# Latent attention with the softmax exponentials issued one head earlier on ScalarE, the query scaling and the spreading of the sums moved there from GpSimd, and finer waits ahead of the scores

## The chip, the cores and the metric

The program runs on one core of one Trainium2 chip. The metric is the device time in microseconds of that core for one execution of the whole program. A core has five engines that each work through a queue of their own in program order: TensorE (PE in the profile, with its weight loads as PEld), VectorE (DVE), ScalarE (ACT), GpSimd (POOL) and SyncE (SP, which issues DMAs). They wait for each other by semaphores.

## The reference, cut to what matters

Two transformer blocks follow each other on a sequence of 1024 tokens of width 1024, all in float32. The change lies in one stage of the second block, the attention over the latent tokens and 256 context tokens:

```
h  = modulate(rmsnorm(x), shift, scale)               # 1024 tokens; hc the same for 256 context tokens
q  = rope(rmsnorm(h @ Wq) * g_q)                      # 8 heads of 128
k, v = those of hc and h, one after the other         # 1280 keys, 2 key heads of 128
for each block of 128 queries and each head:
    s = (q @ k.T) / sqrt(128)                         # 128 x 1280
    y = softmax(s) @ v
```

The projections ahead of this stage and behind it, the two mixers of the first block, the pooling mixer and the feed-forward parts are not touched.

## The kernel before

Products on TensorE are taken in three parts: each float32 operand is split into a high part, which TensorE reads as it is, and a low part, what is left; high x high, high x low and low x high are added up in PSUM. So whatever is transposed on TensorE is read twice from PSUM: by ScalarE, which writes the high part (a copy that rounds), and then by VectorE, which subtracts it and so gives the low part.

The function `latent_attention` (L1298) walks over 8 tiles of 128 queries (`walk`, L1351: the first and the last tile written out, the six between as a hardware loop) and in each over 8 heads. The heads have a running number n from 0 to 63. Two halves of PSUM, three banks each, serve even and odd heads in turn: a half holds first the 1280 scores of its head, and then, in the same banks, the ten transposed 128x128 blocks of its probabilities, in three groups of 4, 4 and 2 blocks. What each engine does for head n, in its order:

- TensorE: transposes the probabilities of head n (L1409), for even heads also the spread reciprocals of the sums (L1402); then one half of the product with the values for the pair of heads before (L1427 to L1429, 15 matmuls); then the scores of head n+2 (`scores`, L1384; its matmuls are L1393 to L1395) in three parts of 512, 512 and 256 keys, which overwrite the banks of the transposed probabilities of head n. For that it waits on the semaphore `probs_t_dve`: before the first part until VectorE has written low groups 0 and 1 of head n, before the third until it has written group 2.
- ScalarE: writes the high parts of the three groups of head n (L1555), for even heads with the copy of the turned factors (L1542) between groups 1 and 2; then the exponentials of head n+1 (`exps`, L1527, its instruction L1531), whose maximum has been there for most of a head.
- VectorE: for odd n the reciprocal of the sums (L1615); the low parts of the three groups (L1629); now and then a piece of the next tile's queries; for odd n the product with the factors (L1620); then the largest score of head n+2 and its negative (L1609, L1611).
- GpSimd: for odd n, the reciprocals spread over 128 columns (`spread_sums`, L1494, its instruction L1498).

The queries of the next tile are made ready on the side, piece by piece: squares on ScalarE in head 0 (L1537), sums on VectorE in head 1 (L1581), the reciprocal root (L1466, L1469) and the scaling of the rows by it (`query_scale`, L1471, L1477) on GpSimd in head 2, the gain on VectorE in head 3 (L1592), the rotation on VectorE and GpSimd in heads 4 and 5 (L1597, L1598, L1604; L1483, L1484, L1492). In head 6 TensorE transposes them in two lots of four heads (`turn_queries`, L1372, its instruction L1381), through one bank: the second lot waits until ScalarE (L1525) and VectorE (L1576) have taken the first, and the scores of the next tile's first head wait for both.

Of the kernel before, what the change touches and what calls it, by code (L numbers as in the profile page):

```python
# [15 lines left out]
ALU = mybir.AluOpType  # L16
ACT = mybir.ActivationFunctionType
# [5 lines left out]
TILES = 8  # L23
# [10 lines left out]
HD2 = 128  # L34
QH2, KV2 = 8, 2
# [172 lines left out]
def bcast(ap, n):  # L208

    return ap.unsqueeze(2).broadcast_to([ap.shape[0], ap.shape[1], n])  # L210
# [1087 lines left out]
def latent_attention(core, q, columns, gain, gain_dram, rotary, kT_hi, kT_lo, v, v_low, ahead):  # L1298
# [15 lines left out]
    with ExitStack() as st:  # L1314
# [18 lines left out]
        with nc.Block() as block:  # L1333
# [28 lines left out]
            def pair_of(t, h):  # L1362
                return t * (QH2 // 2) + h // 2 - 1
# [7 lines left out]
            def _(pe):  # L1371
# [12 lines left out]
                def scores(pe, n, t, h, first=False):  # L1384
                    if h % 4 == 0:
                        pe.wait_ge(core.kq_out_dve.sem, core.kq_out_dve.at(2 * t + 1 + h // 4))
                    g = h // rep
                    for part, (a, b) in enumerate(PARTS):
                        if not first and part != 1:

                            pe.wait_ge(core.probs_t_dve.sem, core.probs_t_dve.at(3 * (n - 2) + (2 if part == 0 else 3)))
                        out = s_bank(h % 2)[:, a:b]
                        nc.tensor.matmul(out, qT_hi[:, h], kT_hi[:, g, a:b], start=True, stop=False)  # L1393
                        nc.tensor.matmul(out, qT_hi[:, h], kT_lo[:, g, a:b], start=False, stop=False)
                        last = nc.tensor.matmul(out, qT_lo[:, h], kT_hi[:, g, a:b], start=False, stop=True)  # L1395
                    last.then_inc(core.scores.sem, 1)
# [63 lines left out]

            @block.gpsimd
            def _(pool):
                def query_rstd(t):
                    pool.wait_ge(core.sums.sem, core.sums.at(t + 1))
                    pool.nop(nofuse=True)
                    pool.tensor_scalar(qrs[:], qsum[:], 1.0 / HD2, EPS, ALU.mult, ALU.add).then_inc(core.links_pool.sem, 1)  # L1466
                    pool.wait_ge(core.links_pool.sem, core.links_pool.at(t + 1))
                    pool.nop(nofuse=True)
                    pool.tensor_tensor(qrs[:], qrs[:], core.minus_half[:, 0:QH2], ALU.pow).then_inc(core.rstd.sem, 1)  # L1469

                def query_scale(t):  # L1471
                    row3, scaled3 = (x.rearrange("p (h d) -> p h d", d=HD2) for x in (q(t), scaled[:]))
                    pool.wait_ge(core.rstd.sem, core.rstd.at(t + 1))
                    pool.nop(nofuse=True)
                    pool.wait_ge(core.rot_dve.sem, core.rot_dve.at(3 * t))
                    pool.nop(nofuse=True)
                    pool.tensor_tensor(scaled3, row3, bcast(qrs[:], HD2), ALU.mult).then_inc(core.hidden.sem, 1)  # L1477

                def query_turn(t):
                    cos, sin = turn_tables(rotary, t, QH2)  # L1480
                    pool.wait_ge(core.staged.sem, core.staged.at(t + 1))
                    pool.nop(nofuse=True)
                    pool.tensor_tensor(product[2][:], b_in, cos, ALU.mult).then_inc(core.rot_pool.sem, 1)  # L1483
                    pool.tensor_tensor(product[3][:], a_in, sin, ALU.mult).then_inc(core.rot_pool.sem, 1)  # L1484

                def query_turned(t):
                    pool.wait_ge(core.rot_pool.sem, core.rot_pool.at(2 * t + 2))
                    pool.nop(nofuse=True)
                    if not isinstance(t, int) or t > 0:
                        pool.wait_ge(core.kq_turned.sem, core.kq_turned.at(2 * t))  # L1490
                        pool.nop(nofuse=True)
                    pool.tensor_tensor(b_out, product[2][:], product[3][:], ALU.add).then_inc(core.kq_rows.sem, 1)  # L1492

                def spread_sums(p, s):  # L1494
                    pool.wait_ge(core.links_dve.sem, core.links_dve.at(p + 1))
                    pool.nop(nofuse=True)
                    for x in range(2):
                        last = pool.tensor_scalar(spread[:, x], core.ones[:], rtotal[:, 2 * s + x:2 * s + x + 1], None, ALU.mult)  # L1498
                    last.then_inc(core.one_over.sem, 1)

                def tile(pool, t, first, more):
                    for h in range(QH2):
                        if more and h == 2:
                            query_rstd(t + 1)
                            query_scale(t + 1)
                        if more and h == 4:
                            query_turn(t + 1)
                        if more and h == 5:
                            query_turned(t + 1)
                        if h % 2:  # L1510
                            spread_sums(pair_of(t, h) + 1, (h // 2) % 2)
                query_rstd(0)
                query_turn(0)
                query_turned(0)
                pool.wait_ge(core.values_high.sem, core.values_high.at(1))
                pool.nop(nofuse=True)
                pool.tensor_tensor(v_low[:], v, v_hi[:].bitcast(F32), ALU.subtract).then_inc(core.values_low.sem, 1)
                walk(pool, tile)
                ahead.first_splits(pool)

            @block.scalar
            def _(act):
                def q_high(act, t, c):
                    act.wait_ge(core.kq_turned.sem, core.kq_turned.at(2 * t + c + 1))
                    act.activation(qT_hi[:, 4 * c:4 * c + 4], q_bank, ACT.Copy).then_inc(core.kq_hi.sem, 1)  # L1525

                def exps(act, n, h):  # L1527

                    act.wait_ge(core.mins.sem, core.mins.at(n + 1))
                    b, q4 = h % 2, h % 4  # L1530
                    act.activation(pr[:, b], s_bank(b)[:, 0:KEYS], ACT.Exp, bias=nb[:, b:b + 1], scale=SCALE,  # L1531
                                   accum_out=total[:, q4:q4 + 1]).then_inc(core.probs.sem, 1)

                def query_squares(t):
                    if not isinstance(t, int) or t > 0:
                        act.wait_ge(core.sums.sem, core.sums.at(t))
                    act.activation(squares[:], q(t), ACT.Square).then_inc(core.sq.sem, 1)  # L1537

                def take_factors(p):
                    if not isinstance(p, int) or p > 0:  # L1540
                        act.wait_ge(core.heads_out.sem, core.heads_out.at(p))
                    act.activation(factors[:], factor_bank, ACT.Copy).then_inc(core.parts_act.sem, 1)  # L1542

                def tile(act, t, first, more):
                    for h in range(QH2):
                        n = t * QH2 + h
                        some = not (first and h < 2)
                        for g in range(3):
                            act.wait_ge(core.probs_t.sem, core.probs_t.at(3 * n + g + 1))
                            if g == 0 and not (first and h < 4):  # L1550

                                act.wait_ge(core.pv.sem, core.pv.at(pair_of(t, h)))
                            if g == 2 and some and h % 2 == 0:
                                take_factors(pair_of(t, h))
                            act.activation(pt(pT_hi, h, g), by_tiles(pt_bank(h % 2, g)), ACT.Copy).then_inc(core.probs_t_act.sem, 1)  # L1555
                        if more or h + 1 < QH2:
                            exps(act, n + 1, (h + 1) % QH2)
                        if more and h == QH2 - 2:
                            q_high(act, t + 1, 0)
                            q_high(act, t + 1, 1)  # L1560
                        if more and h == 0:
                            query_squares(t + 1)
                query_squares(0)
                act.activation(v_hi[:], v, ACT.Copy).then_inc(core.values_high.sem, 1)
                q_high(act, 0, 0)
                q_high(act, 0, 1)
                exps(act, 0, 0)
                walk(act, tile)
                act.wait_ge(core.probs_t.sem, core.probs_t.at(3 * heads + 1))
                take_factors(heads // 2 - 1)  # L1570
# [81 lines left out]
    n = heads  # L1652
# [1973 lines left out]
```

## Time and profile before

| | us |
|---|---|
| device time, median of 3 runs | 3812.06 |
| lowest and highest of the 3 | 3809.18, 3813.14 |
| the profiled execution's own time | 3812.06 |
| its span, first to last instruction | 3810.3 |

Busy over the whole span: TensorE 91%, its weight loads 80%, VectorE 58%, ScalarE 46%, GpSimd 37%. These are means over many stages with different limits; the stage of the change lies between about 1737 and 2104 us of the span. "Idle before" in a row is the time in which the engine did nothing ahead of that row, and the name behind the arrow is what ended it.

### The profile page before, as it was taken

How to read it: one execution, taken by the hardware profiler on the slowest of the kernel's cores; microseconds unless marked ns; L12 is line 12 of the kernel's file. 1: busy time of each engine (PE TensorE's matmuls, PEld its weight loads, DVE VectorE, ACT ScalarE, POOL GpSimd, SP SyncE). 2: the span in 40 equal slices, each digit the busy share in tenths (PEclk: the TensorE clock that was granted, in tenths of full speed). 3: DMA queues.
4: the chain of work that ended last, by engine and by line, in shares of the span. 5: the costliest groups of instructions: out<-in, count | busy, mean ns of one | idle time of the engine just before them, and what ended most of it. 6: DMA issues, size and time to landing. Idle time of an engine off the chain costs nothing. (4 is left out here: it accounts for less than half of the span.)

```text
span 3810.3 us, 59174 instructions
## 1 busy us (share of the span) xinstructions
PE 3464.8 (91%) x18690; PEld 3042.7 (80%) x18690; DVE 2214.7 (58%) x4502; ACT 1740.2 (46%) x4132; POOL 1401.2 (37%) x1828
## 2 busy tenths in 40 slices
PE   5999988899999999797999929999999949999998
PEld 4899877899999987586888727888787748888786
DVE  5466767355677775435777175666435566666334
ACT  1277511667777771324555153333334463333333
POOL 2365323455566763313331334444001224444000
PEclk8999989899999998898999959999999769999999
DMA  3311255211122214300000022222354012222354
GB/s 145 127 40 39 101 221 220 87 42 42 59 62 64 63 61 160 129 1 28 1 0 0 22 107 76 83 83 83 127 197 150 29 49 83 83 83 83 127 198 143
DMA packets 97166, 332.99 MB, mean 87 GB/s; under 512 B 10673, under 2 KB 37601, under 8 KB 85090
## 3 DMA queue, kind: packets, MB, share of 16 engines
q1 hardware_dynamic: 96994, 330.90, 24.5%
q8 instruction: 83, 1.36, 0.2%
q14 instruction: 89, 0.73, 0.1%
HBM read 269.76 MB, written 61.10 MB: 87 GB/s over the span
## 5 line engine op out<-in xcount | busy, mean ns | idle before, releaser
L2062 PE MATMUL ps<-down_high,hidden_high 128*128 128x512 f32 x704 | 277.3, 394 | 13.5 <-DVE hidden_low L1963 13.2
L2045 PE MATMUL ps<-columns_combined,up_high_even 128*128 128x512 f32 x616 | 243.7, 396 | 46.4 <-POOL up_low_even L1830 32.7
L2063 PE MATMUL ps<-down_low,hidden_high 128*128 128x512 f32 x704 | 275.8, 392 | 0.0
L2064 PE MATMUL ps<-down_high,hidden_low 128*128 128x512 f32 x704 | 275.5, 391 | 0.0
L374 PE MATMUL ps<-w_hi,hT_hi 128*128 128x512 f32 x640 | 254.2, 397 | 22.5 <-DVE hT_lo L398 11.9
L1961 DVE TENSOR_TENSOR down_low<-down_raw,down_high 128x1024 fp32r<-128x1024 f32 x88 | 107.8, 1225 | 273.4 <-ACT down_high L1878 273.4
L375 PE MATMUL ps<-w_lo,hT_hi 128*128 128x512 f32 x640 | 252.8, 395 | 0.0
L376 PE MATMUL ps<-w_hi,hT_lo 128*128 128x512 f32 x640 | 252.1, 394 | 0.0
L2046 PE MATMUL ps<-columns_combined,up_high_even 128*128 128x512 f32 x616 | 242.9, 394 | 0.0
L2047 PE MATMUL ps<-columns_combined,up_low_even 128*128 128x512 f32 x616 | 242.5, 394 | 0.0
L2046 PE MATMUL ps<-columns_combined,up_high_odd 128*128 128x512 f32 x616 | 239.7, 389 | 0.0
L2047 PE MATMUL ps<-columns_combined,up_low_odd 128*128 128x512 f32 x616 | 239.7, 389 | 0.0
L2045 PE MATMUL ps<-columns_combined,up_high_odd 128*128 128x512 f32 x616 | 239.7, 389 | 0.0
L1089 ACT ACTIVATE masked_then_probs<-masked_then_probs,unit_rows 128x256 f32<-128x256 f32 (+1 forms) x512 | 229.1, 451 | 3.2 <-DVE sink_term L1176 1.8
L1878 ACT ACTIVATE down_high<-down_raw 128x1024 fp32r<-128x1024 f32 x88 | 93.1, 1058 | 269.6 <-PE ps L2064 257.2
L1026 PEld LDWEIGHTS ps<-v_tiles,probsT 128*128 128x128 f32 x1600 | 203.4, 198 | 1.3 <-issue 1.3
L971 PE MATMUL ps<-w_units,hT_hi 128*128 128x384 f32 (+1 forms) x512 | 184.7, 361 | 18.3 <-DVE w_units L1135 12.5
L1026 PE MATMUL ps<-v_tiles,probsT 128*128 128x64 f32 x1600 | 199.9, 277 | 0.6 <-DVE unit_rows L1249 0.6
L973 PE MATMUL ps<-w_units,hT_lo 128*128 128x384 f32 (+1 forms) x576 | 199.4, 346 | 0.0
L1167 DVE CUSTOM_DVE_ANT_0 masked_then_probs<-ps,mask 128x256 f32<-128x256 f32 (+1 forms) x512 | 156.2, 359 | 60.5 <-PE ps L988 60.1
L2460 DVE SCALAR_TENSOR_TENSOR mod_sums<-mod_weights,silu_c,mod_sums 128x512 f32 x196 | 184.7, 954 | 6.0
L971 PE MATMUL ps<-w_units,hT_hi_by_fours 128*128 128x384 f32 (+1 forms) x512 | 183.6, 359 | 0.2 <-ACT z L1116 0.2
(365 smaller groups left out, 9999.4 us busy)
## 6 DMA issues: line engine op xcount, KB each, us to landing
mod_weights<-in_w_mod SPq DMA_DIRECT2D x24, 2048.0 KB, 8.5
up_raw<-in_w_up SPq DMA_DIRECT2D x44, 1024.0 KB, 4.8
down_raw<-in_w_down SPq DMA_DIRECT2D x88, 512.0 KB, 3.6
hidden_columns<-hidden SPq DMA_DIRECT2D x44, 512.0 KB, 2.6
hidden_columns<-hidden_columns SPq DMA_DIRECT2D x88, 256.0 KB, 3.9
w_raw<-in_w_in_b SPq DMA_DIRECT2D x24, 768.0 KB, 4.5
group_rows<-unit_rows SPq DMA_DIRECT2D x64, 132.0 KB, 1.8
unit_rows<-group_rows SPq DMA_DIRECT2D x64, 132.0 KB, 2.1
```

The lines of the kernel that those rows point to most:

```text
L374: nc.tensor.matmul(out, a, w_hi[:, s], start=(k == 0), stop=False)
L375: nc.tensor.matmul(out, a, w_lo[:, s], start=False, stop=False)
L376: last = nc.tensor.matmul(out, b, w_hi[:, s], start=False, stop=(k == KT - 1))
L971: nc.tensor.matmul(zbank, hi, weights(w_hi, a.unit, k), start=(k == 0), stop=False)
L1026: last = nc.tensor.matmul(o_bank[:, h * HD:(h + 1) * HD], pT[:, a.par, h, c], vs[:, tile], start=(c == a.slots[0]), stop=(c == a.slots[-1]))
L1089: act.activation(x, x, ACT.Exp, bias=own, scale=-1.0, accum_out=total).then_inc(core.probs.sem, 1)
L2045: nc.tensor.matmul(out, a_hi, combined.moving(0, z, k), start=(start and k == 0), stop=False, **again)
L2046: nc.tensor.matmul(out, a_hi, combined.moving(1, z, k), start=False, stop=False, **again)
L2047: last = nc.tensor.matmul(out, a_lo, combined.moving(0, z, k), start=False, stop=(k == 3), **again)
L2062: nc.tensor.matmul(out, h_hi[:, s, t], down_hi[:, s, cols], start=begin, stop=False)
L2063: nc.tensor.matmul(out, h_hi[:, s, t], down_lo[:, s, cols], start=False, stop=False)
L2064: last = nc.tensor.matmul(out, h_lo[:, s, t], down_hi[:, s, cols], start=False, stop=end)
```

## The change

Four things are changed, all in `latent_attention`.

1. `exps` is issued one head earlier. ScalarE starts with the exponentials of heads 0 and 1, and in head n, behind the high parts of head n, it issues those of head n+2 in place of those of head n+1. In head 6 the high parts of the turned queries now stand ahead of the exponentials.
2. The scaling of the queries moves from GpSimd (one instruction, 128x1024) to ScalarE (eight instructions of 128x128, each with its head's scale), into head 2 behind the exponentials.
3. The spreading of the reciprocals moves from GpSimd to ScalarE, into odd heads between the high parts and the exponentials. GpSimd is left with the reciprocal root and its part of the rotation, without the walk over heads; it also comes earlier to the first splits of the next projection's weights.
4. The scores wait for `probs_t_dve` before each of the three parts: for low group 0, 1 and 2 in turn.

```diff
@@ scores, TensorE
                     for part, (a, b) in enumerate(PARTS):
-                        if not first and part != 1:
-
-                            pe.wait_ge(core.probs_t_dve.sem, core.probs_t_dve.at(3 * (n - 2) + (2 if part == 0 else 3)))
+                        if not first:
+
+                            pe.wait_ge(core.probs_t_dve.sem, core.probs_t_dve.at(3 * (n - 2) + part + 1))
@@ GpSimd
-                def query_scale(t):
...
-                    pool.tensor_tensor(scaled3, row3, bcast(qrs[:], HD2), ALU.mult).then_inc(core.hidden.sem, 1)
...
-                def spread_sums(p, s):
...
-                walk(pool, tile)
+                with pool.Fori(1, TILES) as t:
+                    queries(t)
                 ahead.first_splits(pool)
@@ ScalarE
+                def query_scale(t):
+                    act.wait_ge(core.rstd.sem, core.rstd.at(t + 1))
+                    act.wait_ge(core.rot_pool.sem, core.rot_pool.at(2 * t))
+                    act.wait_ge(core.rot_dve.sem, core.rot_dve.at(3 * t))
+                    act.nop(nofuse=True)
+                    for h in range(QH2):
+                        last = act.activation(scaled[:, h * HD2:(h + 1) * HD2], q(t)[:, h * HD2:(h + 1) * HD2], ACT.Copy, scale=qrs[:, h:h + 1])
+                    last.then_inc(core.hidden.sem, 1)
+
+                def spread_sums(p, s):
+                    act.wait_ge(core.links_dve.sem, core.links_dve.at(p + 1))
+                    for x in range(2):
+                        last = act.activation(spread[:, x], core.ones[:], ACT.Copy, scale=rtotal[:, 2 * s + x:2 * s + x + 1])
+                    last.then_inc(core.one_over.sem, 1)
@@ ScalarE, tile, at the end of head h
-                        if more or h + 1 < QH2:
-                            exps(act, n + 1, (h + 1) % QH2)
+                        if h % 2:
+                            spread_sums(pair_of(t, h) + 1, (h // 2) % 2)
                         if more and h == QH2 - 2:
                             q_high(act, t + 1, 0)
                             q_high(act, t + 1, 1)
+                        if more or h + 2 < QH2:
+                            exps(act, n + 2, (h + 2) % QH2)
                         if more and h == 0:
                             query_squares(t + 1)
+                        if more and h == 2:
+                            query_scale(t + 1)
@@ ScalarE, ahead of the walk
                 exps(act, 0, 0)
+                exps(act, 1, 1)
```

ScalarE's queue in heads 1 to 3 of the first tile, before: `probsT_high` are the high parts, `probs,sums` the exponentials. The two rows of `probs,sums` are the exponentials of heads 2 and 3.

```order
L1555 ACTIVATE probsT_high<-ps 128x4x128 [waits probs_t] x2
L1555 ACTIVATE probsT_high<-ps 128x2x128 [waits probs_t]
L1531 ACTIVATE probs,sums<-ps,minus_largest 128x1280 [waits mins]
L1555 ACTIVATE probsT_high<-ps 128x4x128 [waits probs_t] x2
L1542 ACTIVATE factors_by_query<-ps 128x256 [waits probs_t]
L1555 ACTIVATE probsT_high<-ps 128x2x128
L1531 ACTIVATE probs,sums<-ps,minus_largest 128x1280 [waits mins]
L1555 ACTIVATE probsT_high<-ps 128x4x128 [waits probs_t] x2
```

The same place in the changed kernel, where line numbers differ; the rows of `probs,sums` are now the exponentials of heads 3 and 4.

```order
L1540 ACTIVATE probsT_high<-ps 128x2x128 [waits probs_t]
L1521 ACTIVATE one_over_sums_spread<-ones,one_over_sums 128x128 [waits links_dve]
L1521 ACTIVATE one_over_sums_spread<-ones,one_over_sums 128x128
L1501 ACTIVATE probs,sums<-ps,minus_largest 128x1280 [waits mins]
L1540 ACTIVATE probsT_high<-ps 128x4x128 [waits probs_t] x2
L1527 ACTIVATE factors_by_query<-ps 128x256 [waits probs_t]
L1540 ACTIVATE probsT_high<-ps 128x2x128
L1501 ACTIVATE probs,sums<-ps,minus_largest 128x1280 [waits mins]
L1515 ACTIVATE scaled_queries<-x,query_rstd 128x128 [waits rot_dve,rstd,rot_pool]
L1515 ACTIVATE scaled_queries<-x,query_rstd 128x128 x7
L1540 ACTIVATE probsT_high<-ps 128x4x128 [waits probs_t] x2
```

The order of high parts and exponentials is the same in shape, but each exponential belongs to one head later, and spreading and scaling now stand in the same queue.

TensorE's scores of one head in the changed kernel, first tile. Before, the second row of 128x512 with L1393 had no wait, and the rest reads the same.

```order
L1393 MATMUL ps<-kT_hi,qT_hi 128x512 [waits probs_t_dve]
L1394 MATMUL ps<-kT_lo,qT_hi 128x512
L1395 MATMUL ps<-kT_hi,qT_lo 128x512
L1393 MATMUL ps<-kT_hi,qT_hi 128x512 [waits probs_t_dve]
L1394 MATMUL ps<-kT_lo,qT_hi 128x512
L1395 MATMUL ps<-kT_hi,qT_lo 128x512
L1393 MATMUL ps<-kT_hi,qT_hi 128x256 [waits probs_t_dve]
```

There is one wait more in a head's scores, and the first asks for one low group where it asked for two.

## Rows read from the trace of the kernel before

**Rows 1.** Stretch view: one tile; busy time of each engine, then PEclk.
```profile
core 0: us, PE busy (x) PEld busy (x) DVE busy (x) ACT busy (x) POOL busy (x), PEclk, DMA share, GB/s
...
1932.02:1975.42 43.40, 40.63 (x290) 36.94 (x289) 33.58 (x56) 24.58 (x47) 12.34 (x14) 1.00 0.00 0
```

**Rows 2.** View of waits, 1760 to 2100 us: who waited for whom, in total.
```profile
ACT probsT_high L1555 <- PE ps L1409: 134.7, 64, 2.6
...
PEld ps L1393 <- DVE probsT_low L1629: 22.2, 45, 2.2
...
PEld ps L1381 <- DVE qT_lo L1576: 10.0, 7, 1.4
```

**Rows 3.** Timeline of the first heads: start, duration, engine, line, operation, count, idle before.
```profile
1756.90 1.49 DVE L1609 TENSOR_REDUCE largest<-ps 128x1 f32<-128x1280 f32 x1 [1.88 <-PE ps L1395]
...
1758.43 0.15 DVE L1611 TENSOR_SCALAR minus_largest<-largest 128x1 f32<-128x1 f32 x1
1758.62 1.33 ACT L1531 ACTIVATE probs<-ps,minus_largest 128x1280 f32<-128x1280 f32 x1 [4.32 <-DVE minus_largest L1611]
...
1760.21 0.15 DVE L1611 TENSOR_SCALAR minus_largest<-largest 128x1 f32<-128x1 f32 x1
1760.79 1.36 ACT L1555 ACTIVATE probsT_high<-ps 128x512 fp32r<-128x512 f32 x3 [0.75 <-PE ps L1409]
1761.41 1.62 DVE L1629 TENSOR_TENSOR probsT_low<-ps,probsT_high 128x512 fp32r<-128x512 f32 x3 [1.05 <-ACT probsT_high L1555]
...
1762.76 0.50 PE L1393 MATMUL ps<-kT_hi,qT_hi 128*128 128x512 f32 x1 [1.35 <-DVE probsT_low L1629]
...
1764.81 1.49 DVE L1609 TENSOR_REDUCE largest<-ps 128x1 f32<-128x1280 f32 x1 [1.78 <-PE ps L1395]
```

**Rows 4.** Timeline, head 6 of a tile, ScalarE's own.
```profile
1920.19 1.09 ACT L1555 ACTIVATE probsT_high<-ps 128x512 fp32r<-128x512 f32 x2 [2.56 <-PE ps L1409]
...
1921.68 1.36 ACT L1531 ACTIVATE probs<-ps,minus_largest 128x1280 f32<-128x1280 f32 x1
...
1922.99 0.63 ACT L1525 ACTIVATE qT_hi<-ps 128x512 fp32r<-128x512 f32 x1
```

**Rows 5.** Timeline, heads 0 and 1: squares on ScalarE, VectorE's odd head.
```profile
1891.93 1.09 ACT L1537 ACTIVATE query_squares<-x 128x1024 f32 x1
...
1895.85 1.62 DVE L1629 TENSOR_TENSOR probsT_low<-ps,probsT_high 128x512 fp32r<-128x512 f32 x3
...
1898.51 0.41 DVE L1620 TENSOR_TENSOR x<-ps,factors_by_query 128x256 f32 x1
```

**Rows 6.** Timeline of ScalarE in other stages: small scaled activations.
```profile
905.78 1.29 ACT L1069 ACTIVATE scaled<-z,head_rstd 128x64 f32<-128x64 f32 x5
906.97 0.46 ACT L1077 ACTIVATE squares<-z 128x320 f32<-128x320 f32 x1
...
3080.00 2.88 ACT L3074 ACTIVATE pool_columns<-ps,modulation,pre_gain_ffn 128x128 f32<-128x128 f32 x8
```

**Rows 7.** Timeline, head 6: the turned queries' low part and TensorE.
```profile
1923.64 0.69 DVE L1576 TENSOR_TENSOR qT_lo<-ps,qT_hi 128x512 fp32r<-128x512 f32 x1 [0.70 <-ACT qT_hi L1525]
...
1924.39 0.66 PE L1381 MATMUL ps<-identity,q_rows 128*128 128x128 f32 x4 [1.24 <-DVE qT_lo L1576]
1924.80 0.48 PE L1393 MATMUL ps<-kT_hi,qT_hi 128*128 128x512 f32 x1
```

**Rows 8.** Timeline: the last two heads' high parts.
```profile
2092.94 1.09 ACT L1555 ACTIVATE probsT_high<-ps 128x512 fp32r<-128x512 f32 x2 [2.35 <-PE ps L1409]
...
2096.62 1.36 ACT L1555 ACTIVATE probsT_high<-ps 128x512 fp32r<-128x512 f32 x3 [0.74 <-PE ps L1409]
```

**Rows 9.** Stretches of 4 us, columns as in rows 1.
```profile
1764.00:1768.00 4.00, 2.06 (x16) 1.75 (x15) 3.15 (x7) 3.09 (x6) 1.20 (x2) 1.00 0.00 0
...
2924.00:2928.00 4.00, 4.00 (x12) 3.15 (x11) 3.97 (x4) 0.00 (x0) 0.00 (x0) 0.57 0.88 267
```

**Rows 10.** Timeline of TensorE: after an idle time, and the very first scores.
```profile
2923.38 0.50 PE L2062 MATMUL ps<-down_high,hidden_high 128*128 128x512 f32 x1 [2.91 <-DVE hidden_low L1963]
...
1753.32 0.78 PE L1393 MATMUL ps<-kT_hi,qT_hi 128*128 128x512 f32 x1
```

More of the change, by code:

```diff
@@ L1462, in _, with queries @@
             def _(pool):
-                def query_rstd(t):
+                def queries(t, first=False):
+                    cos, sin = turn_tables(rotary, t, QH2)
                     pool.wait_ge(core.sums.sem, core.sums.at(t + 1))
@@ L1469, in query_rstd @@
                     pool.tensor_tensor(qrs[:], qrs[:], core.minus_half[:, 0:QH2], ALU.pow).then_inc(core.rstd.sem, 1)
-                def query_scale(t):
[L1472 to L1476, printed above, removed]
-                    pool.tensor_tensor(scaled3, row3, bcast(qrs[:], HD2), ALU.mult).then_inc(core.hidden.sem, 1)
-                def query_turn(t):
-                    cos, sin = turn_tables(rotary, t, QH2)
                     pool.wait_ge(core.staged.sem, core.staged.at(t + 1))
@@ L1484, in query_turn @@
                     pool.tensor_tensor(product[3][:], a_in, sin, ALU.mult).then_inc(core.rot_pool.sem, 1)
-                def query_turned(t):
                     pool.wait_ge(core.rot_pool.sem, core.rot_pool.at(2 * t + 2))
                     pool.nop(nofuse=True)
-                    if not isinstance(t, int) or t > 0:
+                    if not first:
                         pool.wait_ge(core.kq_turned.sem, core.kq_turned.at(2 * t))
@@ L1492, in query_turned @@
                     pool.tensor_tensor(b_out, product[2][:], product[3][:], ALU.add).then_inc(core.kq_rows.sem, 1)
-                def spread_sums(p, s):
[L1495 to L1514, printed above, removed]
+                queries(0, first=True)
                 pool.wait_ge(core.values_high.sem, core.values_high.at(1))
```

## The prediction

> **What bounds the kernel now.** I read the stage by stretches first. One whole tile of eight heads takes 43.40 us, 5.43 us a head; TensorE is busy for 40.63 us of it, 5.08 us a head, at full clock (1.00), and ScalarE for 24.58 only [rows 1]. So TensorE is nearly the bound, and ScalarE has room as a sum. The view of waits says what TensorE's idle time is: in some 340 us its weight loads wait 22.2 us for the low parts ahead of the scores, and 10.0 us at the turned queries [rows 2]. Some 32 us in the whole stage are all that better waits could give. ScalarE's largest wait is 134.7 us, for the transposed probabilities: today it stands ready when TensorE delivers. The reader is to ask of the change whether it still will.
>
> For that the first heads are of use, since nothing covers their steps there, and the chain can be read step by step [rows 3]: largest at 1756.90, its negative at 1758.43, exponentials at 1758.62; high parts at 1760.79, low parts at 1761.41, scores at 1762.76, next largest at 1764.81.
>
> **The change, part by part.**
>
> *The exponentials one head earlier.* In the changed queue the exponentials of head n+2 stand ahead of the high parts of head n+1. They need the largest score of head n+2, and this needs its scores, which TensorE writes just ahead of transposing head n+1. Before, the exponentials at this place had their maximum long since. Now ScalarE waits there with the high parts of head n+1 behind it; VectorE's low parts wait for those, and the scores of head n+3 for the low parts, which closes a loop with one turn a head. What stands in each queue behind the wait is thus the next link of the same loop, and no other work can come forward.
>
> The rule that decides is in the Trainium skill, "TensorE: Matmul & The Clock Gate", section on architectural detail: the queues of ScalarE and VectorE are strictly first in, first out. Were it not so, the high parts could pass the waiting exponentials and the loop would not close; that is the third rival below. The rows show the order kept and no case that would have tempted it.
>
> One turn of the loop, from start to start:
> - scores to largest: 1762.76 to 1764.81, 2.05 [rows 3]
> - largest to its negative: 1756.90 to 1758.43, 1.53 [rows 3]
> - negative to exponentials: 1758.43 to 1758.62, 0.19 [rows 3]
> - exponentials with the reading of their sum, to the next work in the queue: 1921.68 to 1922.99, 1.31 [rows 4]
> - first high part to first low part: 1760.79 to 1761.41, 0.62 [rows 3]
> - first low part to the scores: before, two low groups took 1761.41 to 1762.76, 1.35 [rows 3]; with the finer wait one is enough, 0.69 long by rows 7's instruction of the same shape plus 0.06 to reach TensorE (1923.64 + 0.69 to 1924.39), 0.75 [rows 7]. The later groups follow at the pace of the score parts and cost nothing.
>
> The sum is 6.45 us a head, against 5.08 of work on TensorE, which is left with 1.37 idle. So the finer waits save 0.60 a turn, but inside a loop that is 1.4 longer per head than TensorE's work.
>
> The high parts of head 0 come after both first exponentials: the second can start at 1760.21 + 0.19 = 1760.40 and ends its turn 1.31 later at 1761.71, against 1760.79 before [rows 3]: +0.92. From there to the high parts of head 62 are 62 turns: 62 x 6.45 = 399.9.
>
> *Side work that now stands in the loop*, once for each of the seven next tiles:
> - the squares in head 0 come between exponentials and high parts: 1.09 long, less the overlap of about 0.1 that neighbours in the queue have, 1.0 [rows 5].
> - the scaling, eight activations with a scale by pointer, stands at the same place in head 2. The row of 128x64 gives 5 in 1.19, 0.238 each (905.78 to 906.97) [rows 6], a lower end of 1.90; 128x128 from PSUM with two pointers gives 2.88/8 = 0.36, an upper end of 2.88 [rows 6]. Each column more costs (1.36 - 0.63) / 768 = 0.95 ns, by the exponentials of 1280 and the copy of 512 columns [rows 4]; I take the lower end plus 64 such columns: 0.30 each, 2.39. GpSimd's root and its wait are over by then.
> - the turning of queries in head 6: counted from the first high part of head 6, ScalarE comes to the queries after 1.49 (1920.19 to 1921.68), the first lot takes 0.63 [rows 4], VectorE 0.75 to TensorE and the second lot 0.41 (1924.39 to 1924.80) [rows 7]; with 0.05 for a handover, the scores of the next tile start at 3.33 instead of 0.62 + 0.75 = 1.37: +1.96. The exchange that puts the high parts of the queries ahead of the exponentials is needed for this, and otherwise hidden.
> - VectorE in heads 1, 3 and 4: low parts, a query piece and the product take 1895.85 to 1898.51 and 0.41 more [rows 5], so the largest can start 0.62 + 2.66 + 0.41 = 3.69 after the first high part, where the loop wants it at 0.62 + 0.75 + 2.05 = 3.42: +0.27, three times 0.81.
>
> Together 6.16, times seven 43.1. Spreading the sums (two activations, under 0.4 each by the same rows) costs nothing: it falls into ScalarE's wait for the largest. If the loop were not there it would cost 0.6 in odd heads on an engine that is half idle. GpSimd's relief saves nothing that TensorE waits for, and its splits for the next projection come earlier without being wanted.
>
> *The end.* Head 63 has no exponentials between it and head 62, so its high parts follow after 1.49 [rows 4] where 2092.94 to 2096.62 is 3.68 now [rows 8]: -2.19.
>
> Heads 0 to 62 took 1760.79 to 2092.94, 332.15 [rows 3, 8]. The sum is 0.92 + 399.9 + 43.1 - 332.15 - 2.19 = +109.6.
>
> *TensorE's clock.* After an idle time of 2.91 TensorE started at 2923.38 [rows 10], and the next 4 us show a granted clock of 0.57 although it was busy throughout: mostly the lower level, 1.2 GHz [rows 9]. In the stretch 1764 to 1768 it idled 1.94 of 4 us and kept 1.00, 2.4 GHz [rows 9]. The changed loop idles 1.37 in a plain head, 2.4 at the squares, 3.8 at the scaling and up to 3.3 at the queries, so falls are likely at two places a tile. Cold scores take 1753.32 to 1756.90, 3.58 [rows 3, 10], 1.53 more than 2.05; since the fall in rows 9 comes a good half microsecond after the restart, I take 0.95 a fall: 7 x 2 x 0.95 = 13.3. Bounds: 0, and three whole ones a tile, 32.
>
> All this is against the profiled execution: its own time, 3812.06, has 1.76 outside the span and is also the median of the runs shown. 3812.1 + 109.6 + 13.3 = 3935.0, the forecast. Its own range is 3905 (scaling at 1.90, VectorE never late, no fall of the clock: 3812.1 + 109.6 - 3.4 - 5.7 = 3912.6, and 0.1 less a head for handovers that overlap) to 3965 (32 for the clock, 3.4 for the scaling at 0.36, 0.1 more a head for the loop's register instructions).
>
> **Rivals.**
>
> *The clock falls in every head.* For it: 2.91 of idle sufficed, and no row shows a steady 1.37 in 6.45. Against it: 1.94 idle within 4 us did no harm. Price: 1.53 in each of 62 turns in place of 13.3: 3921.7 + 95 = 4017; if it goes to and fro, half of it, 3969. The Trainium skill, same page, section on the clock gate, has only two levels, and a clock that activity releases. By that rule the price would be all or nothing at each restart; the granted 0.57 and 1.00 of rows 9 agree with two levels.
>
> *Only the loop costs, the side work hides.* If squares, scaling and queries fell into waits: 3812.1 + 0.92 + 399.9 - 332.15 - 2.19 = 3878.6. Against it: they stand between the exponentials and the high parts, where ScalarE is the link of the loop.
>
> *The exponentials don't hold the high parts back.* Then TensorE stays the bound and the finer waits give what they can: 22.2 less ahead of the scores [rows 2], 3790, faster. The place is ScalarE's queue between two heads, and the point that decides is whether 3.03 us (1.53 + 0.19 + 1.31) from the largest to the end of the exponentials fit before the first transposed block is there. TensorE transposes at once behind the scores, and the largest waits for the same scores, so the first transposed block is there while VectorE still looks for the largest; they don't fit. Only if the scores came a head ahead would this hold, and their banks don't allow that.
>
> **How the numbers follow.** The forecast 0.72; the clock in every head or most 0.16; hidden side work 0.06; the faster rival 0.05; anything else 0.01. The predicted time is that of the first. The range reaches down to 3895, for a loop that is shorter than its steps, and up to 3990, past the half of the clock rival, and leaves out less than 2 in 10. About 0.2% is what a measurement of this kernel can tell from no change, 7.6 us; only the third rival lies on the other side: faster 0.05, same 0.01, slower 0.94.
>
> **What would show it.** The first high part of one head to that of the next should be 6.4 to 6.5 us in plain heads (5 and 7), over 7 behind squares and over 8.5 behind the scaling; a tile about 57.8 us (8 x 6.45 + 6.16) plus what the clock takes. ScalarE's largest wait should be for the negative of the largest, where it was for the transposed probabilities, each about 3 to 3.7 us (6.45 less 1.49 for the high parts, 1.31 for the exponentials and up to 0.6 for spreading); the wait of the scores for the low parts should grow from 22.2 to over 80 us, with TensorE's busy time in the stage hardly changed. Granted clock under 1.00 should show behind the scaling. I am wrong if the high parts start while exponentials are outstanding, if plain heads take 5.1 to 5.4 us, or if TensorE idles elsewhere than ahead of the scores.

## The result, and the profile after

| | before | changed |
|---|---|---|
| device time, median of 4 runs | 3810.62 us | 3929.35 us |
| lowest to highest | 3808.26 to 3813.14 | 3924.3 to 3935.17 |
| ratio, with its 95% interval | | 1.0312 (1.0294 to 1.033) |
| span of the profiled execution | 3810.3 us | 3935.0 us |
| the profiled execution's own time | 3812.06 us | 3936.82 us |

The changed kernel is 3.1% slower. The forecast was 3935 with a range of 3895 to 3990. The profiled execution of the changed kernel took 7.5 us more than the median of its other four; the traces below are of that one.

The stretch view of the changed kernel shows one tile, from the first high part of head 7 to that of the next head 7, and single heads of it; columns as in rows 1.

```profile
1935.94:1942.38 6.44, 5.07 (x36) 4.62 (x36) 3.60 (x6) 3.25 (x9) 0.00 (x0) 1.00 0.00 0
...
1965.19:1972.94 7.75, 6.39 (x36) 5.88 (x36) 4.73 (x7) 3.23 (x9) 3.82 (x3) 0.78 0.00 0
...
1935.94:1994.23 58.29, 42.25 (x288) 38.24 (x288) 33.20 (x55) 29.11 (x66) 5.66 (x5) 0.97 0.00 0
```

A tile takes 58.29 us where it took 43.40 [rows 1]. TensorE is busy 42.25 us of it, hardly more than the 40.63 before; most of the 1.6 more is the head at a granted clock of 0.78, busy for 6.39 where the plain head shows 5.07. ScalarE's 29.11 against 24.58 is the work moved to it. Neither engine is full; what grew is waiting. A plain head (first row) lasts 6.44 us.

The view of waits of the changed kernel, 1760 to 2215 us, in the form of rows 2:

```profile
ACT probs L1501 <- DVE minus_largest L1601: 223.7, 62, 5.0
DVE probsT_low L1619 <- ACT probsT_high L1540: 141.6, 62, 4.2
...
PEld ps L1393 <- DVE probsT_low L1619: 107.7, 53, 4.1
...
PEld ps L1381 <- DVE qT_lo L1566: 18.6, 7, 2.7
```

Read downwards this is the loop: the exponentials wait for the largest (62 times, 3.6 us each), the low parts for the high parts behind them, the scores for the low parts, 107.7 us where it was 22.2 [rows 2]. ScalarE's wait for the transposed probabilities, 134.7 us before, is gone from the list: now TensorE has delivered long since, and the high parts lie in the queue.

ScalarE's timeline of the changed kernel through most of that tile (heads 7, 0, 1, 2, 3), columns as in rows 3:

```profile
1935.94 1.35 ACT L1540 ACTIVATE probsT_high<-ps 128x512 fp32r<-128x512 f32 x3
1937.16 0.71 ACT L1521 ACTIVATE one_over_sums_spread<-ones,one_over_sums 128x128 f32<-128x128 f32 x2
1941.06 1.33 ACT L1501 ACTIVATE probs<-ps,minus_largest 128x1280 f32<-128x1280 f32 x1 [3.19 <-DVE minus_largest L1601]
...
1942.38 1.07 ACT L1540 ACTIVATE probsT_high<-ps 128x512 fp32r<-128x512 f32 x2
...
1948.82 1.04 ACT L1507 ACTIVATE query_squares<-x 128x1024 f32 x1
1949.76 1.35 ACT L1540 ACTIVATE probsT_high<-ps 128x512 fp32r<-128x512 f32 x3
...
1956.40 1.07 ACT L1540 ACTIVATE probsT_high<-ps 128x512 fp32r<-128x512 f32 x2
...
1962.86 2.43 ACT L1515 ACTIVATE scaled_queries<-x,query_rstd 128x128 f32 x8
1965.19 1.33 ACT L1540 ACTIVATE probsT_high<-ps 128x512 fp32r<-128x512 f32 x3
...
1972.94 1.08 ACT L1540 ACTIVATE probsT_high<-ps 128x512 fp32r<-128x512 f32 x2
```

From one first high part to the next: 6.44 (plain), 7.38 (squares between), 6.64, 8.79 (scaling between), 7.75 (no work between, but granted clock 0.78). High parts never start while an exponential is outstanding ahead of them. The spreading sits in front of ScalarE's 3.19 us wait and costs nothing.

TensorE's timeline in the changed kernel, the starts of scores that had to wait:

```profile
1943.75 0.50 PE L1393 MATMUL ps<-kT_hi,qT_hi 128*128 128x512 f32 x1 [1.36 <-DVE probsT_low L1619]
1951.13 0.50 PE L1393 MATMUL ps<-kT_hi,qT_hi 128*128 128x512 f32 x1 [2.52 <-DVE probsT_low L1619]
...
1966.55 0.55 PE L1393 MATMUL ps<-kT_hi,qT_hi 128*128 128x512 f32 x1 [3.90 <-DVE probsT_low L1619]
```

1.36 idle in a plain head, 2.52 behind the squares, 3.90 behind the scaling.

### The profile page after: what moved, and what is told of

The parts are those of the page before. It is cut to its first block and busy times, and to the rows that moved or that the text cites. A ratio compares the mean times of both kernels' runs of the same rounds, so it can differ in the third digit from the quotient of the medians.

```text
span 3935.0 us, 59284 instructions
## 1 busy us (share of the span) xinstructions
PE 3494.9 (89%) x18690; PEld 3066.0 (78%) x18690; DVE 2218.2 (56%) x4502; ACT 1774.3 (45%) x4252; POOL 1347.6 (34%) x1757
## 3 DMA queue, kind: packets, MB, share of 16 engines
q8 instruction: 83, 1.36, 0.1%
## 5 line engine op out<-in xcount | busy, mean ns | idle before, releaser
L1501 ACT ACTIVATE probs<-ps,minus_largest 128x1280 f32<-128x1280 f32 x64 | 85.2, 1330 | 231.3 <-DVE minus_largest L1601 231.3
```

## The experiments

Eight kernels took the change apart or shifted one part of it; two more look for a better order. They ran in three groups, each with runs of the kernel before beside it, whose medians were 3813.0, 3808.5 and 3812.7 us; a ratio is always to the kernel before of the same group.

**The exponentials alone.** The kernel before with this edit (and the exponentials of head 1 ahead of the walk):

```diff
-                        if more or h + 1 < QH2:
-                            exps(act, n + 1, (h + 1) % QH2)
                         if more and h == QH2 - 2:
                             q_high(act, t + 1, 0)
                             q_high(act, t + 1, 1)
+                        if more or h + 2 < QH2:
+                            exps(act, n + 2, (h + 2) % QH2)
```

> The kernel before with one part of the change alone: the exponentials one head earlier (heads 0 and 1 ahead of the walk, the turned queries' high parts ahead of the exponentials in head 6). Scaling, spreading and the coarse waits stay as before. Theory of the loop: a plain head lasts 6.44 as in the changed kernel plus 0.60 for the coarser wait, 7.04; squares add 1.0 and the queries 1.36 per tile; 62 x 7.04 + 7 x 2.36 against 332.15 before gives +120, with about 13 for the clock 3943 us, between 3930 and 3975. Rival, the loss comes from the scaling and spreading put on ScalarE: close to before, 3800 to 3820.

Measured: 3953.39 us, ratio 1.0373 (1.0358 to 1.0388). A plain head, in ScalarE's timeline of this kernel:

```profile
1909.51 1.35 ACT L1555 ACTIVATE probsT_high<-ps 128x512 fp32r<-128x512 f32 x3
...
1916.57 1.07 ACT L1555 ACTIVATE probsT_high<-ps 128x512 fp32r<-128x512 f32 x2
```

1909.51 to 1916.57 is 7.06 us, as the loop wants it. This one part makes a loss larger than the whole change's. The 10 us above the expected 3943 are largely the clock's: in this trace 23 heads show a granted clock below 1.00 and are 25 us longer in all than heads of their kind at 1.00, where 13 had been taken.

**The finer waits alone.** The kernel before with the first hunk of the change.

> The kernel before with the three finer waits ahead of the scores alone. Theory of the loop: waits for low parts are only 22.2 us before, and the first score part may start one low group, 0.60, earlier; so 10 to 22 us faster, 3789 to 3800. Rival, the added wait costs something or another engine is late at once: 3805 to 3815.

Measured: 3789.67 us, ratio 0.9945 (0.9933 to 0.9957). The loads' wait for low parts fell from 22.2 to 4.9 us; the 10.0 us at the turned queries stayed. A tile takes 40.6 us (1922.62 to 1963.21) where it took 43.40. The rival falls.

**All but the exponentials.** The changed kernel, with the exponentials back:

```diff
-                        if more or h + 2 < QH2:
-                            exps(act, n + 2, (h + 2) % QH2)
+                        if more or h + 1 < QH2:
+                            exps(act, n + 1, (h + 1) % QH2)
```

> The changed kernel with the exponentials back at their old place (those of head n+1 behind the high parts of head n), while scaling and spreading stay on ScalarE and the waits stay fine. Theory of the loop: plain heads fall to TensorE's 5.0 to 5.2 us, the whole to 3790 to 3812. Rival, ScalarE's added work makes the loss: it stays above 3870.

Measured: 3786.67 us, ratio 0.9933 (0.9921 to 0.9945). A tile of this kernel:

```profile
1932.45:1972.68 40.23, 39.36 (x289) 36.59 (x288) 33.68 (x56) 29.24 (x65) 5.69 (x5) 1.00 0.00 0
```

ScalarE's busy time is that of the changed kernel (29.24 and 29.11), yet the tile takes 40.23 us instead of 58.29, and TensorE is busy 98% of it. So it is not the amount of work on ScalarE, but the place of the exponentials, that makes the loss. With the finer waits this kernel is even faster than the one before. Its interval overlaps with that of the finer waits alone (0.9933 to 0.9957), so with the exponentials at their old place the scaling and the spreading on ScalarE cost nothing that can be told.

**The exponentials between the groups.** The changed kernel with the exponentials of head n+1 behind group 0, and then behind group 1, of the high parts of head n:

```diff
                             act.activation(pt(pT_hi, h, g), by_tiles(pt_bank(h % 2, g)), ACT.Copy).then_inc(core.probs_t_act.sem, 1)
+                            if g == 0 and (more or h + 1 < QH2):      # second kernel: g == 1
+                                exps(act, n + 1, (h + 1) % QH2)
```

> The changed kernel with the exponentials of head n+1 between the first and second group of the high parts of head n, so one group of high parts later than in the changed kernel. Theory of the loop: only score parts 2 and 3 hang on the exponentials now, the first part of 0.70 us leaves the loop: plain heads of 6.44 - 0.70 = 5.74 us, squares and scaling hidden, the whole 3840 to 3860. Rival, ScalarE is late as a whole by what was added to its queue: no change against the changed kernel, 3925 to 3935.

> The changed kernel with the exponentials of head n+1 between the second and third group of the high parts of head n. Theory of the loop: only the last score part (0.35 us) hangs on them, a turn of 4.6 to 4.8 us is shorter than TensorE's work of 5.08, so TensorE is the bound again: 3785 to 3805. Rival, any wait of ScalarE for a fresh maximum ahead of high parts holds TensorE back: over 3820.

Measured: 3857.05 us, ratio 1.0114 (1.0098 to 1.0129), behind group 0; 3801.9 us, ratio 0.9985 (0.9976 to 0.9994), behind group 1. ScalarE's timeline, behind group 0:

```profile
1939.32 0.60 ACT L1540 ACTIVATE probsT_high<-ps 128x512 fp32r<-128x512 f32 x1 [2.02 <-PE ps L1409]
1940.64 1.33 ACT L1501 ACTIVATE probs<-ps,minus_largest 128x1280 f32<-128x1280 f32 x1 [0.71 <-DVE minus_largest L1600]
...
1945.19 0.60 ACT L1540 ACTIVATE probsT_high<-ps 128x512 fp32r<-128x512 f32 x1 [1.80 <-PE ps L1409]
1946.39 1.33 ACT L1501 ACTIVATE probs<-ps,minus_largest 128x1280 f32<-128x1280 f32 x1 [0.60 <-DVE minus_largest L1600]
```

The first group's high part now stands ahead of the exponentials and is no link of the loop, so the turn is read from one exponential to the next: 1940.64 to 1946.39, 5.75 us, where 5.74 was expected. In the last tile, which prepares no queries, the seven turns are 5.74 to 5.76 us.

Behind group 1, two heads of the last tile in the stretch view, and VectorE in a head with a piece of the next queries (the rotation):

```profile
2066.87:2076.33 9.46, 9.46 (x73) 8.77 (x72) 6.93 (x13) 6.42 (x14) 0.00 (x0) 1.00 0.00 0
```

```profile
1909.71 0.42 DVE L1618 TENSOR_TENSOR probsT_low<-ps,probsT_high 128x256 fp32r<-128x256 f32 x1 [0.78 <-ACT probsT_high L1540]
1910.05 0.68 DVE L1586 TENSOR_TENSOR rotation<-scaled_queries,axial 128x512 f32<-128x512 f32 x1
1910.65 0.69 DVE L1587 TENSOR_TENSOR rotation<-scaled_queries,axial 128x512 f32<-128x512 f32 x1
1911.25 1.48 DVE L1598 TENSOR_REDUCE largest<-ps 128x1 f32<-128x1280 f32 x1
```

Plain heads take 6.44 us with the exponentials ahead of all groups, 5.75 behind the first, and 4.73 behind the second (9.46 for two), where TensorE is busy throughout (less than the 5.08 us a head that the prediction read from a whole tile); with the exponentials at their old place a pair of plain heads takes 9.45 us in the last tile. So the loop shrinks by what no longer hangs on it, until TensorE's own work is longer.

Still this order stays 15 to 20 us (by medians and by ratios) behind the old place with the same waits. The loss lies in the seven tiles that prepare queries: one takes 42.44 us (1882.62 to 1925.06) against 40.23, and seven times 2.2 is 15.5. From head 1 to head 5 of that tile the exponentials follow each other at 5.15 to 5.25 us. In one of these four turns ScalarE is busy throughout, with the scaling. In the others VectorE has a query piece; in the rows above it waits 0.78 us for the high part behind the exponentials, and then goes through the low part, the piece and the next largest without a pause. So a smaller loop between ScalarE and VectorE is left, and the expected rival holds in part.

**The coarse waits back.** The changed kernel without its first hunk.

> The changed kernel with the old coarse waits ahead of the scores. Theory of the loop: each turn is longer by a low group of 0.60: 7.04 in plain heads, 62 x 0.60 = 37 less what it saves where VectorE or the queries are late (about 4 a stage each): 3955 to 3975. Rival, the waits don't matter since ScalarE sets the pace: no change, 3929.

Measured: 3970.78 us, ratio 1.0421 (1.0405 to 1.0437), by the medians 41 us over the changed kernel. Plain heads take 7.05 us (1926.79 to 1933.84 on ScalarE), 0.61 more. Not every turn pays that: the head of the turned queries keeps its 8.38 us, and behind squares and scaling 7.05 stands against 6.64. That makes some 31 us in 62 heads; the clock takes most of the rest, as 25 heads below 1.00 lose 27 us in this trace against 18 heads and 18 us in that of the changed kernel. In the kernel before the same edit was worth 23 us against its group's median, since there it removed only waits.

**The scaling back on GpSimd.** The changed kernel with the one instruction of 128x1024 behind the root on GpSimd, in place of the eight on ScalarE.

> The changed kernel with the scaling of the queries alone back on GpSimd as one instruction of 128x1024. Theory of the loop: 2.35 less per tile and, with that idle time gone, no fall of the clock behind it (1.0 per tile): 7 x 3.35 = 23 us faster than the changed kernel, 3906; the head behind head 2 lasts 6.44 to 6.7. Rival, the scaling hides in ScalarE's wait for the largest: no change, 3929.

Measured: 3905.25 us, ratio 1.0253 (1.0238 to 1.0269), 24 us less than the changed kernel. The head that held the scaling takes 6.45 us (1941.07 to 1947.52 on ScalarE), the one behind it 6.65. The rival falls: work between exponentials and high parts is paid in full. The clock still falls behind the squares in four of the seven tiles, as it does in the changed kernel; one tile that shows it:

```profile
1933.12:1941.07 7.95, 6.59 (x36) 5.87 (x36) 4.72 (x7) 3.24 (x9) 3.74 (x3) 0.79 0.00 0
1947.52:1954.17 6.65, 5.10 (x36) 4.62 (x36) 4.64 (x7) 3.25 (x10) 2.77 (x3) 1.00 0.00 0
```

In the two traces the stage differs by 30.0 us (461.98 against 491.94): seven times 2.34 for the scaling, and 13.5 because the clock fell in 6 heads where it fell in 18. The medians lie only 24 us apart, and the profiled execution of the changed kernel was a long one; so how often the clock falls seems to differ between executions of one kernel, which no further trace here shows.

**TensorE kept busy behind the scaling.** The changed kernel with this:

```diff
+                        if more and h == 3:
+                            for n_ in range(28):
+                                nc.tensor.transpose(q_bank[:, n_ % 4], core.ident[:], core.ident[:])
                         if more or h + 2 < QH2:
                             scores(pe, n + 2, t + (h + 2) // QH2, (h + 2) % QH2)
```

> The changed kernel with 28 extra transposes of the identity on TensorE (about 3 us) into the unused query bank, ahead of the scores of head 3, where TensorE idles 3.8 us behind the scaling. Their results are not used. If the clock makes the head behind the scaling 7.75 us long instead of 6.44 + 0.27: it falls to about 6.7, some 1 us a tile or 7 us in all, 3922, with a granted clock of 1.00 there. If it is VectorE or the rows' own noise: no change in that head.

Measured: 3921.51 us, ratio 1.0294 (1.0278 to 1.0309). The median is 7.8 us under that of the changed kernel, but the two intervals overlap, so what is shown is shown by the trace. TensorE's transposes and its next scores, ScalarE's timeline around the scaling, and the stretch of the head behind it:

```profile
1960.43 3.22 PE L1447 MATMUL ps<-identity 128*128 128x128 f32 x28
1964.49 0.50 PE L1393 MATMUL ps<-kT_hi,qT_hi 128*128 128x512 f32 x1 [0.84 <-DVE probsT_low L1622]
```

```profile
1960.80 2.43 ACT L1518 ACTIVATE scaled_queries<-x,query_rstd 128x128 f32 x8
1963.14 1.32 ACT L1543 ACTIVATE probsT_high<-ps 128x512 fp32r<-128x512 f32 x3
...
1969.77 1.07 ACT L1543 ACTIVATE probsT_high<-ps 128x512 fp32r<-128x512 f32 x2
```

```profile
1963.14:1969.77 6.63, 5.58 (x41) 4.88 (x39) 4.64 (x7) 3.23 (x8) 2.77 (x3) 1.00 0.00 0
```

The same head takes 6.63 instead of 7.75 us and the granted clock is 1.00 instead of 0.78. So 1.12 us of that head were the clock's, and 0.19 VectorE's. It is so in every tile: all seven heads behind the scaling take 6.63 or 6.64 us at 1.00, where in the changed kernel all seven are below 1.00 and take 6.86 to 8.00.

**Better orders.** Two kernels keep the old place of the exponentials and the finer waits, and put the high part of the first lot of queries ahead of the exponentials in head 6, that of the second lot behind them; the first leaves scaling and spreading on GpSimd, the second has them on ScalarE.

```diff
                         if more and h == QH2 - 2:
                             q_high(act, t + 1, 0)
                         if more or h + 1 < QH2:
                             exps(act, n + 1, (h + 1) % QH2)
+                        if more and h == QH2 - 2:
                             q_high(act, t + 1, 1)
```

> The kernel before with the three finer waits, and in head 6 the high part of the first lot of turned queries ahead of the exponentials (of the old place), that of the second lot behind them. With the finer waits alone TensorE still waits 10.0 us for the turned queries in seven tiles; the exponentials, 1.31, leave that wait. Expected 7 x 1.3 = 9 us less than the finer waits alone, 3781, between 3776 and 3786. Rival, TensorE then waits for the exponentials of head 7 at once: no gain, 3790.

> The changed kernel with the exponentials at their old place and, in head 6, between the two lots of the turned queries' high parts instead of behind both. With both lots ahead, TensorE waits 5.2 us in all for exponentials and 4.5 us for the queries; the former should go. Expected 3 to 6 us less than with both lots ahead (3786.7), 3780 to 3784. Rival, the second lot is late in its turn and TensorE waits there as long: no gain.

Measured: 3785.47 us, ratio 0.9933 (0.9919 to 0.9947), and 3779.31 us, ratio 0.9923 (0.9909 to 0.9936). In the second the loads' wait for exponentials fell from 5.2 to 2.3 us. It is the fastest kernel run here, 33 us under its group's median of the kernel before; its interval overlaps with the one of all but the exponentials, so by the medians the split of the two lots alone is not shown to gain. The first gained 4 us where 9 were expected, and its interval overlaps with that of the finer waits alone as well. The traces are clearer: from the exponentials of one head to those of the same head in the next tile are 39.8 us in both kernels, with the finer waits alone 40.6 and in all but the exponentials 40.2, in each of the tiles between the first and the last. In the first kernel the loads' wait at the turned queries fell only from 10.0 to 4.5 us, not to nothing as the expected 9 us would need.

## Why the prediction was right

The mechanism was the one forecast, and its steps can be set beside the trace of the changed kernel.

- *The loop's turn*: forecast 6.45, measured 6.44. The rows of the first heads gave every link, since they had run there without cover. With the coarse wait, 0.60 more by the forecast, a plain head took 7.05 and 7.06.
- *Squares, scaling, queries*: forecast 1.0, 2.39 and 1.96; measured 0.94 (7.38 - 6.44), 2.33 (1962.86 to 1965.19) and 1.95 (the last head of the tile, 1985.84 to 1994.23, less 6.44). The lengthening of the small activations from a narrower row was sound.
- *VectorE late in heads 1, 3 and 4*: forecast 0.27 each; measured 0.20 and 0.19 in heads 1 and 3, nothing in head 4 of that tile, though the prediction had counted its two products like the others without a row for them. Together 3 us too much in the stage. One head 4 was late all the same, where GpSimd, freed by the change, already splits the next projection's weights; the prediction had put that at nothing. VectorE's two products (before the dots in the usual tile, behind them in this one, with one of GpSimd's splits) took 1.12 and 1.76 us instead of 0.68 and 0.69, and the head 7.90 us (2149.95 to 2157.85) at a granted clock of 1.00, 1.45 more; with GpSimd's work left as it was (the exponentials alone) the same head took 7.05 like its plain ones. The rows show this; what slowed the two instructions was not tested.

```profile
1975.10 0.68 DVE L1587 TENSOR_TENSOR rotation<-scaled_queries,axial 128x512 f32<-128x512 f32 x1
1975.69 0.69 DVE L1588 TENSOR_TENSOR rotation<-scaled_queries,axial 128x512 f32<-128x512 f32 x1
...
2152.11 1.12 DVE L1587 TENSOR_TENSOR rotation<-scaled_queries,axial 128x512 f32<-128x512 f32 x1
2152.82 1.53 POOL L249 TENSOR_TENSOR w_lo<-w_raw,w_hi 128x512 fp32r<-128x512 f32 x1
2153.15 1.76 DVE L1588 TENSOR_TENSOR rotation<-scaled_queries,axial 128x512 f32<-128x512 f32 x1
```

- *The clock*: forecast 14 falls at 0.95, 13.3 us. The trace shows a granted clock below 1.00 in 18 of 62 heads: seven of seven behind the scaling, six of seven at the turned queries, four of seven behind the squares, and the first head. Set against heads of their kind at 1.00 they are 18.3 us longer in all, 1.02 each. At the two places that the prediction named, scaling and queries, 13 falls cost 13.1 us, as forecast. What it left out are the falls behind the squares (4.3 us) and in the first head (1.0), so the term is 5 us too small.
- *The sum*: from the first high part (1759.99) to that of head 62 (2218.89) are 458.9 us, against 456.3 forecast (443.0 without the clock). The clock is 5.0 more and the GpSimd head 1.45; VectorE's lateness is 3.0 less, squares, scaling and queries together 0.8 less. That the total fits to 3 us is thus partly luck, since misses of both signs met. In the two profiled executions the stage, from ScalarE's first squares to its first copy of the next stage, lasts 491.94 (1735.87 to 2227.81) and 368.03 us (1737.74 to 2105.77); the difference is 123.9, where 122.9 was forecast. The median of the runs lies 5.7 under the forecast. Four executions of the changed kernel differ by 11 us, but so do those of the kernel before, by 13 us in eleven, so nothing can be read from that.
- *The rivals*: the clock didn't fall in every head; all plain heads show 1.00. Nor did a restart cost all or nothing, as the prediction had drawn from the two levels: the seven heads behind the scaling lost from 0.2 to 1.4 us, each running in part at either level (granted clock 0.57 to 0.79 over the head). The side work did not hide, as the scaling on GpSimd shows. ScalarE's strict queue, which the Trainium skill gives under "TensorE: Matmul & The Clock Gate", section on architectural detail, held in every row: three places of the exponentials in the queue gave three lengths of a head.
- *The finer waits*: taken as worth up to 22 us if TensorE stayed the bound; alone they gave 23 against their group's median (21 by the ratio 0.9945).

## What to carry to other kernels

In a queue that is strictly in order, issuing an instruction earlier makes everything behind it wait for that instruction's operands: before moving one ahead, ask what it will wait for there, and whether what stands behind it feeds, through other engines, the next turn of the same wait. If so, add up the loop from rows where its links ran uncovered, and compare it with the busiest engine's work per turn; work put between two links is then paid in full, however idle its engine is. The finer waits paid in either kernel here, 23 us where TensorE was the bound and 41 in the loop.

## What the runs showed that was not expected

Extra work made a head shorter: some 3 us of transposes without a use took 1.12 us off the head that followed, because TensorE then met the scores at the full clock. Over the seven tiles that is 6.6 us, as the seven heads had lost from 0.2 to 1.4 us each; the medians differ by 7.8, though the intervals don't separate the two kernels.

The same idle time does not always end the same way. In the changed kernel TensorE is idle 2.52 us ahead of the scores behind the squares in one tile and again in another, shown with the result (1951.13):

```profile
1830.89 0.80 PE L1393 MATMUL ps<-kT_hi,qT_hi 128*128 128x512 f32 x1 [2.52 <-DVE probsT_low L1619]
```

The first head shows a granted clock of 0.78 and 7.75 us, the second 1.00 and 6.64. And a change in one head moves the falls in others, as the count over all 62 heads of one trace each shows:

| kernel | heads below 1.00 | us they are longer |
|---|---|---|
| the changed kernel | 18 | 18.3 |
| TensorE kept busy behind the scaling | 11 | 10.8 |
| the scaling back on GpSimd | 6 | 4.8 |
| the exponentials alone | 23 | 25.1 |
| the coarse waits back | 25 | 27.0 |

With the scaling on GpSimd the clock fell at the turned queries in one tile of seven, where the changed kernel shows six.
